# Narrower GpSimd roots, a later evacuation of an expert's result, and a fifth slot of split weights in a two-block float32 transformer kernel

## The chip, the cores and the metric

The kernel runs on one core of one Trainium2 chip. The metric is the device time of one execution in microseconds (us); lower is better. Engines: TensorE (PE, its weight loads PEld) multiplies, VectorE (DVE) and ScalarE (ACT) work elementwise and can read the accumulator PSUM, GpSimd (POOL) works elementwise in SBUF, SyncE (SP) issues most DMAs.

## The reference, cut to what matters

256 tokens of width 1024 pass through a first block (two layers of SwiGLU, a mixer of RWKV and retention heads, SwiGLU) and a second block (two layers of a mixer, cross attention to a memory, a mixture of 16 experts). Everything is float32.

```
def rms_norm(x, gain, eps=NORM_EPS):
    y = xf * lax.rsqrt(jnp.mean(xf * xf, axis=-1, keepdims=True) + eps)
def layer_norm(x, g, b):
    y = (xf - mu) * lax.rsqrt(var + LN_EPS) * g + b
def grouped_moe(...):                      # top 2 of 16 experts for each token
    for e in range(N_EXPERTS):
        he = jax.nn.silu(xt @ w_gate[e]) * (xt @ w_up[e])      # 1024 -> 512
        y = y + combine[:, e:e + 1] * (he @ w_down[e])         # 512 -> 1024
```

The first block has seven RMS norms of whole rows (three a layer and a final one). Inside a layer there are also roots for the key vectors (8 heads of 2 tiles, 16 columns), for the retention heads (8 columns) and for the RWKV heads of each tile (8 columns). The second block has six layer norms and one norm over 8 groups of 2 tiles (16 columns).

## The kernel before, in words

**Rows and columns.** The 256 tokens are two tiles (NT = 2) of 128 partitions. The root of a row norm is therefore 2 columns of 128: one value for each tile and partition. A head norm of one tile is RH = 8 columns.

**Split weights.** Each float32 matmul is done as three: a weight block `raw` (128 x 1024, 512 KB) is rounded by ACT to `whi`, DVE subtracts it from `raw` to give `wlo`, and PE multiplies `whi` with the high part of the data, `wlo` with the high part and `whi` with the low part. SP loads the next `raw` block when DVE is done with an old one.

**Roots.** DVE puts the variances into `rs_in` (16 columns) and raises `rs_asked`; GpSimd computes `rs_in ** -0.5` over all 16 columns into `rs_out` and raises `rs_given`; DVE waits for that in `rsqrt(n)` and scales. 22 such roots run in a fixed order: RSQ = 7 in each of two layers (0: first norm, 1: mixer norm, 2: keys, 3: retention heads, 4 and 5: RWKV heads of tile 0 and 1, 6: second feed-forward norm), then the final norm, the group norm, and six layer norms. In `rms` DVE does nothing while it waits; in `layer_norm` it does two scalar_tensor_tensor operations of its own in the meantime. After a norm PE transposes the normed rows (`turn_rows`), ACT and DVE evacuate them as `xTh` and `xTl`, and the next matmuls start. While a norm runs, PE executes `keep_busy`, a number of matmuls on zeros, ahead of `turn_rows` in its queue.

**Experts.** In each layer of the second block three experts are computed over all tokens and the other NR = 13 over their own tokens only (CAPS: at most 128, 104, 88, ... 32 rows). For those 13 the weights come in NC = 156 chunks: for round i four chunks `up` and four chunks `gate` of expert i, then four chunks `down` of expert i - 1. PE's order in round i is: up(i), `scatter(i - 2)` (which adds an expert's result to the tokens), gate(i), down(i - 1), `turn_e(i)` (transposes of the hidden rows). Split chunks go through NW = 4 slots (three of `whi`/`wlo`, and `w3h`/`w3l`); ACT's split of chunk n waits until PE has used chunk n - NW. ACT and DVE run one program each, in the same order (`split_e`, `silu_e`/`gated_e`, `hidden_e`, `out_e`):

```
                    if i < NR:
                        if i:
                            split_e()
                            if i > 1:
                                out_e(i - 2)
                            split_e()
                            if i == 1:
                                silu_e(0)
                            hidden_e(i - 1)
                        for _ in range(6):
                            split_e()
```

`out_e(i - 2)` copies the down result of expert i - 2 from two PSUM banks into `outh` (stored in `xTh`) and, on DVE, the low half into `outl` (in `xTl`); it needs the last down chunk of the round before. `hidden_e(i - 1)` does the same with the transposed hidden rows (`hTh`, `hTl`) and needs `turn_e(i - 1)`.

Of the kernel before, what the change touches and what calls it, by code (L numbers as in the profile page):

```python
# [8 lines left out]
F32R = mybir.dt.float32r  # L9
BF16 = mybir.dt.bfloat16  # L10
I32 = mybir.dt.int32
ALU = mybir.AluOpType
# [4 lines left out]
P = 128  # L17
D = 1024
S = 256
NT = S // P  # L20
# [51 lines left out]
UNIT_BANKS = (0, 1, 2, 3, 5, 6)  # L72
TURN_BANKS = (0, 1, 2, 3, 5, 6, 7)
NC = 12 * NR
NRAW, NW = 6, 4
UB, GB = 4, 5
POOLS = (2, 4, 8, 16)

# [60 lines left out]
def both_blocks(nc, A, out):  # L139
    ctx = ExitStack()  # L140
    with ctx:
# [51 lines left out]
        xgl = at("xgl", [P, KB, SLOTS], F32R, offset=RB_at)  # L193
        w3h = at("w3h", [P, 1024], F32R, offset=tl_at)
        w3l = at("w3l", [P, 1024], F32R, offset=tl_at + 4 * 1024)
        outh = xTh[:].rearrange("p k s -> p (k s)")[:, 0:D]
        outl = xTl[:].rearrange("p k s -> p (k s)")[:, 0:D]
        gsf, hrows = (b[:].rearrange("p j s -> p (j s)") for b in (gs, h32))
# [240 lines left out]

        def e_w(n):  # L440

            return (w3h[:], w3l[:]) if n % NW == 3 else (whi[:, n % NW], wlo[:, n % NW])

        def hold(eng, signal, value):

# [194 lines left out]
        @block.gpsimd  # L640
        def _(pool):
            pool.wait_ge(setup, 3)

            def rsqrt(n):
                pool.wait_ge(rs_asked, n + 1)
                nc.gpsimd.tensor_tensor(rs_out[:], rs_in[:], neg_half[:], ALU.pow).then_inc(rs_given, 1)  # L646

            with pool.Fori(0, DEPTH) as l:
                for n in range(2):
                    rsqrt(RSQ * l + n)  # L650

                nc.gpsimd.memset(prev[0:1, 0], 0.0).then_inc(zero_row, 1)
                rsqrt(RSQ * l + 2)

                for t in range(NT):
                    for lev in range(6):
                        for hf in range(2):
                            hs = slice(4 * hf, 4 * hf + 4)
                            if lev == 0:

                                pool.wait_ge(L_ready, 16 * l + 8 * t + 4 * hf + 4)
                                if t:

                                    pool.wait_ge(q_psum, 24 * l + 12)
                            else:

                                pool.wait_ge(q_psum, 24 * l + 12 * t + 2 * lev - 2 + hf + 1)
                                if lev == 1:
                                    pool.wait_ge(t_ready, 24 * l + 12 * t + hf + 1)
                            mask = tab[:, T_LEV + lev * P:T_LEV + (lev + 1) * P]  # L670
                            nc.gpsimd.tensor_tensor(Aoff[:, hs], Lm[:, hs, 0:P], mask.unsqueeze(1).to_broadcast([P, 4, P]),  # L671
                                                    ALU.mult).then_inc(aoff_ready, 1)
                    rsqrt(RSQ * l + 3 + t)
                for n in range(5, RSQ):
                    rsqrt(RSQ * l + n)
            with pool.Fori(RSQ * DEPTH, RSQ * DEPTH + 8) as n:
                rsqrt(n)

        @block.scalar
        def _(act):  # L680
# [45 lines left out]
            def experts(l):  # L726
# [32 lines left out]
                for i in range(NR + 1):  # L759
                    if i < NR:  # L760
                        if i:
                            split_e()
                            if i > 1:
                                out_e(i - 2)
                            split_e()
                            if i == 1:
                                silu_e(0)
                            hidden_e(i - 1)
                        for _ in range(6):
                            split_e()  # L770
                        if i:
                            split_e()
# [249 lines left out]
        def _(dve):  # L1022
# [494 lines left out]
            def experts(l):  # L1517
# [119 lines left out]
                for i in range(NR + 1):  # L1637
                    if i < NR:
                        if i:
                            split_e()  # L1640
                            if i > 1:
                                out_e(i - 2)
                            split_e()
                            if i == 1:
                                gated_e(0)
                            hidden_e(i - 1)
                        for c in range(6):
                            split_e()
                            if i == 0 and c == 1:
                                add(ND - 1)  # L1650
# [729 lines left out]
```

## Time and profile before

| | |
|---|---|
| median of 3 runs | 2846.18 us (2845.74 to 2848.23) |
| the profiled execution | 2848.95 us, its span 2847.1 us |
| PE, DVE, ACT, POOL busy | 90%, 58%, 41%, 5% of the span |
| granted TensorE clock, mean | 0.956 of full speed |
| DMA | 460 MB, 162 GB/s over the span |

A row of a timeline is: start in us, duration in us, engine, line, operation, out<-in, count, and in square brackets the idle time before it with what ended it. The span starts at 0.

### The profile page before, as it was taken

The page shows a single profiled execution, that of the slowest core. Times are in us where ns is not written, and L with a number is a line of the kernel's source. Part 1 is how long each engine was busy: PE and PEld are TensorE (multiplying, and loading weights), DVE is VectorE, ACT ScalarE, POOL GpSimd, SP SyncE. Part 2 cuts the span into 40 slices and gives each one's busy share as a digit, 9 for nine tenths or more (in the row PEclk, how much of TensorE's full clock was granted, in tenths as well). Part 3 has the DMA queues.
Part 4 walks back from the last instruction along what each step waited for, and adds up shares of the span by engine and source line. Part 5 has one row for each costly group of instructions (what it writes and reads, how often), then busy time and mean ns, then how long its engine had stood idle before and what let it go on. Part 6 is the DMA issues. An engine that isn't in the chain of part 4 may idle for free.

```text
span 2847.1 us, 39605 instructions
## 1 busy us (share of the span) xinstructions
PE 2561.4 (90%) x14872; PEld 2068.0 (73%) x14872; DVE 1650.0 (58%) x1993; ACT 1153.6 (41%) x1338; POOL 137.4 (5%) x76
## 2 busy tenths in 40 slices
PE   8998888999999888899997889999997877999996
PEld 7987786898898778689885767985443665985443
DVE  5555754554555575455543446667776445667776
ACT  4543312343454331244331323446664321446663
POOL 0000131000000022100000000000000000000000
PEclk9999999999999999999998899999998998999998
DMA  6674201666466520166652323668885422568884
GB/s 212 179 219 141 91 1 30 177 190 179 139 186 199 162 70 1 37 185 184 183 156 85 119 74 114 178 211 305 293 290 192 132 89 60 149 207 297 296 288 168
DMA packets 387417, 460.37 MB, mean 162 GB/s; under 512 B 18534, under 2 KB 272978, under 8 KB 387154
## 3 DMA queue, kind: packets, MB, share of 16 engines
q1 hardware_dynamic: 382384, 448.64, 50.0%
q10 hardware_dynamic: 4898, 9.95, 1.2%
q8 instruction: 83, 1.36, 0.2%
q14 instruction: 52, 0.43, 0.0%
HBM read 453.83 MB, written 1.05 MB: 160 GB/s over the span
## 4 chain that ended last, share of the span: by engine, by line
issue 86%; PE 9%; DVE 2%; POOL 2%; DMA 1%; ACT 0%; ACTq 0%; POOLq 0%; DVEq 0%
PE PS L1951 1%; PE PS L1953 1%; PE PS L1952 1%; POOL rs_out L646 1%; PE PS L2079 1%; POOL solve_b L671 1%; PE PS L2089 1%; DMA RA<-proj 1%; PE PS L2088 1%; PE PS L2062 0%; PE PS L2063 0%; PE PS L2067 0%; DVE solve_a L1282 0%; DVE wlo L1135 0%; PE PS L2120 0%
## 5 line engine op out<-in xcount | busy, mean ns | idle before, releaser
L1084 DVE TENSOR_TENSOR wlo<-raw,whi 128x1024 fp32r<-128x1024 f32 x336 | 410.2, 1225 | 392.6 <-ACT whi L696 391.9
L696 ACT ACTIVATE whi<-raw 128x1024 fp32r<-128x1024 f32 x336 | 355.3, 1060 | 537.0 <-PE PS L1759 361.4
L1757 PE MATMUL PS<-xTh,whi 128*128 128x256 f32 x1792 | 508.7, 284 | 1.7 <-ACT xgh L1011 1.7
L1758 PE MATMUL PS<-xTl,whi 128*128 128x256 f32 x1792 | 507.7, 283 | 0.0
L1759 PE MATMUL PS<-xTh,wlo 128*128 128x256 f32 x1792 | 507.6, 283 | 0.0
L1757 PEld LDWEIGHTS PS<-xTh,whi 128*128 128x128 f32 x1792 | 344.4, 192 | 7.3 <-issue 3.2
L1758 PEld LDWEIGHTS PS<-xTl,whi 128*128 128x128 f32 x1792 | 344.4, 192 | 4.1
L1759 PEld LDWEIGHTS PS<-xTh,wlo 128*128 128x128 f32 x1792 | 344.2, 192 | 0.0
L1612 DVE TENSOR_TENSOR wlo<-raw,whi 128x1024 fp32r<-128x1024 f32 x234 | 280.6, 1217 | 71.8 <-ACT whi L739 71.6
L739 ACT ACTIVATE whi<-raw 128x1024 fp32r<-128x1024 f32 x234 | 245.9, 1054 | 96.1 <-PE PS L1862 78.0
L1951 PE MATMUL PS<-whi,xTh 128*128 128x416 f32 (+2 forms) x544 | 212.6, 391 | 39.5 <-DVE xTl L1064 18.9
L1953 PE MATMUL PS<-whi,xTl 128*128 128x416 f32 (+2 forms) x544 | 207.1, 381 | 0.0
L1952 PE MATMUL PS<-wlo,xTh 128*128 128x416 f32 (+2 forms) x544 | 206.8, 380 | 0.0
L1078 DVE TENSOR_TENSOR wlo<-raw,whi 128x1024 fp32r<-128x1024 f32 (+2 forms) x92 | 106.6, 1177 | 153.5 <-ACT whi L707 152.1
L646 POOL TENSOR_TENSOR rs_out<-rs_in,neg_half 128x16 f32<-128x16 f32 x22 | 71.4, 3244 | 2521.1 <-DVE rs_in L1355 1329.3
L1773 PE MATMUL PS<-whi,hTh 128*128 128x512 f32 x448 | 178.3, 398 | 10.4 <-DVE wlo L1084 10.4
L1774 PE MATMUL PS<-wlo,hTh 128*128 128x512 f32 x448 | 177.7, 397 | 0.0
L1775 PE MATMUL PS<-whi,hTl 128*128 128x512 f32 x448 | 176.5, 394 | 0.0
L1860 PE MATMUL PS<-whi,xgh 128*36 128x512 f32 (+11 forms) x312 | 127.0, 407 | 43.9 <-DVE wlo L1612 43.8
L707 ACT ACTIVATE whi<-raw 128x1024 fp32r<-128x1024 f32 (+2 forms) x92 | 90.8, 1016 | 179.5 <-PE PS L1953 122.6
L1951 PEld LDWEIGHTS PS<-whi,xTh 128*128 128x128 f32 x544 | 106.7, 196 | 65.2 <-issue 28.4
L1729 PE MATMUL PS<-zero 128*128 128x512 bf16 x536 | 124.0, 391 | 10.7 <-issue 9.0
(424 smaller groups left out, 4452.9 us busy)
## 6 DMA issues: line engine op xcount, KB each, us to landing
raw<-in_l_e_gate_dram SPq DMA_DIRECT2D x128, 512.0 KB, 4.7
raw<-in_l_e_up_dram SPq DMA_DIRECT2D x128, 512.0 KB, 5.8
raw<-in_l_e_down_dram SPq DMA_DIRECT2D x128, 512.0 KB, 5.3
raw<-in_ffn_w_gate_dram SPq DMA_DIRECT2D x88, 512.0 KB, 5.0
raw<-in_ffn_w_up_dram SPq DMA_DIRECT2D x88, 512.0 KB, 6.1
raw<-in_ffn_w_down_dram SPq DMA_DIRECT2D x88, 512.0 KB, 3.4
raw<-in_w_in_dram SPq DMA_DIRECT2D x64, 416.0 KB, 3.9
raw<-in_l_xkv_dram SPq DMA_DIRECT2D x32, 512.0 KB, 3.8
```

The source lines that it names most:

```text
L696: nc.scalar.activation(whi[:, m], raw[:, m, j], ACT.Copy).then_inc(hi_done[m], 1)
L739: nc.scalar.activation(e_w(n)[0], e_raw(n), ACT.Copy).then_inc(e_hi, 1)
L1084: nc.vector.tensor_tensor(wlo[:, m], raw[:, m, j], whi[:, m].bitcast(F32), ALU.subtract).then_inc(lo_done[m], 1)
L1612: TTop(e_w(n)[1], e_raw(n), e_w(n)[0].bitcast(F32), ALU.subtract).then_inc(e_lo, 1)
L1757: mm(out_, whi[:, m, ks], xTh[:, k, :], start=(k == 0), stop=False)
L1758: mm(out_, whi[:, m, ks], xTl[:, k, :], start=False, stop=False)
L1759: last = mm(out_, wlo[:, m, ks], xTh[:, k, :], start=False, stop=(k == KB - 1))
L1773: mm(out_, hTh[:, j, ts], whi[:, 2, ns], start=(opens is not None), stop=False, skip_group_check=True)
L1774: mm(out_, hTh[:, j, ts], wlo[:, 2, ns], start=False, stop=False, skip_group_check=True)
L1951: mm(out_, of[0][:, k, ts], whi[:, at[c], ws], start=(k == 0), stop=False)
L1952: mm(out_, of[0][:, k, ts], wlo[:, at[c], ws], start=False, stop=False)
L1953: last = mm(out_, of[1][:, k, ts], whi[:, at[c], ws], start=False, stop=(k == KB - 1))
```

## The change

1. GpSimd's `rsqrt(n, c0, c1)` takes the root only over the columns that the norm has: 2 for each row norm and layer norm (13 roots), 8 for retention and RWKV heads (6 roots), 16 as before for the keys and the group norm (3 roots).
2. In the order of ACT and DVE, `out_e(i - 2)` moves from behind the first `up` split of round i to behind the third; `hidden_e(i - 1)`, still behind the second, now comes before it.
3. NW is 5: a fifth slot `w4h`/`w4l` of split weights lies where `xn` is (which the experts don't use).

```
-NRAW, NW = 6, 4
+NRAW, NW = 6, 5
+        w4h = at("w4h", [P, 1024], F32R, offset=xn_at)
+        w4l = at("w4l", [P, 1024], F32R, offset=xn_at + 4 * 1024)
-            return (w3h[:], w3l[:]) if n % NW == 3 else (whi[:, n % NW], wlo[:, n % NW])
+            if n % NW < 3:
+                return whi[:, n % NW], wlo[:, n % NW]
+            return (w3h[:], w3l[:]) if n % NW == 3 else (w4h[:], w4l[:])
...
-            def rsqrt(n):
+            def rsqrt(n, c0, c1):
                 pool.wait_ge(rs_asked, n + 1)
-                nc.gpsimd.tensor_tensor(rs_out[:], rs_in[:], neg_half[:], ALU.pow).then_inc(rs_given, 1)
+                nc.gpsimd.tensor_tensor(rs_out[:, c0:c1], rs_in[:, c0:c1], neg_half[:, c0:c1], ALU.pow).then_inc(rs_given, 1)
                 for n in range(2):
-                    rsqrt(RSQ * l + n)
+                    rsqrt(RSQ * l + n, 0, NT)
-                rsqrt(RSQ * l + 2)
+                rsqrt(RSQ * l + 2, 0, 16)
-                    rsqrt(RSQ * l + 3 + t)
-                for n in range(5, RSQ):
-                    rsqrt(RSQ * l + n)
-            with pool.Fori(RSQ * DEPTH, RSQ * DEPTH + 8) as n:
-                rsqrt(n)
+                    rsqrt(RSQ * l + 3 + t, 0, RH)
+                rsqrt(RSQ * l + 5, RH, 2 * RH)
+                rsqrt(RSQ * l + 6, 0, NT)
+            rsqrt(RSQ * DEPTH, 0, NT)
+            rsqrt(RSQ * DEPTH + 1, 0, 16)
+            with pool.Fori(RSQ * DEPTH + 2, RSQ * DEPTH + 8) as n:
+                rsqrt(n, 0, NT)
...
                         if i:
                             split_e()
-                            if i > 1:
-                                out_e(i - 2)
                             split_e()
                             if i == 1:
                                 silu_e(0)
                             hidden_e(i - 1)
-                        for _ in range(6):
+                            split_e()
+                            if i > 1:
+                                out_e(i - 2)
+                        for _ in range(5 if i else 6):
                             split_e()
```

(The last piece stands twice, for ACT as here and for DVE with `gated_e`.)

DVE in round i = 8 of layer 0, where the results have 52 rows and the hidden rows 192 columns; `wlo`, `w3l`, `w4l` are splits of chunks, `xTl` is `out_e(6)`, `hTl` is `hidden_e(7)`. Before:

```order
806 L1618 SCALAR_TENSOR_TENSOR h<-gs,par,PS 48x512
807 L1612 TENSOR_TENSOR wlo<-raw,whi 128x1024
808 L1612 TENSOR_TENSOR w3l<-raw,w3h 128x1024
809 L1612 TENSOR_TENSOR wlo<-raw,whi 128x1024
810 L1629 TENSOR_TENSOR xTl<-PS,xTh 52x1024
811 L1612 TENSOR_TENSOR wlo<-raw,whi 128x1024
812 L1624 TENSOR_TENSOR hTl<-PS,hTh 128x192
813 L1612 TENSOR_TENSOR wlo<-raw,whi 128x1024
814 L1612 TENSOR_TENSOR w3l<-raw,w3h 128x1024
```

The same place on DVE with the change:

```order
803 L1625 SCALAR_TENSOR_TENSOR h<-gs,par,PS 48x512
804 L1619 TENSOR_TENSOR wlo<-raw,whi 128x1024 x3
805 L1619 TENSOR_TENSOR w3l<-raw,w3h 128x1024
806 L1631 TENSOR_TENSOR hTl<-PS,hTh 128x192
807 L1619 TENSOR_TENSOR w4l<-raw,w4h 128x1024
808 L1636 TENSOR_TENSOR xTl<-PS,xTh 52x1024
809 L1619 TENSOR_TENSOR wlo<-raw,whi 128x1024 x3
```

Behind the hidden rows' gating (the first row) DVE now does four splits (down 2, down 3, up 0, up 1) before it turns to the hidden rows, then the third up split, then the result; before, the result stood between up 0 and up 1. ACT's queue moved in the same way. Before:

```order
496 L744 ACTIVATE gs<-PS 48x512
497 L739 ACTIVATE whi<-raw 128x1024
498 L739 ACTIVATE w3h<-raw 128x1024
499 L739 ACTIVATE whi<-raw 128x1024
500 L752 ACTIVATE xTh<-PS 52x1024
501 L739 ACTIVATE whi<-raw 128x1024
502 L748 ACTIVATE hTh<-PS 128x192
503 L739 ACTIVATE whi<-raw 128x1024
```

And ACT with the change:

```order
493 L750 ACTIVATE gs<-PS 48x512
494 L745 ACTIVATE whi<-raw 128x1024 x3
495 L745 ACTIVATE w3h<-raw 128x1024
496 L754 ACTIVATE hTh<-PS 128x192
497 L745 ACTIVATE w4h<-raw 128x1024
498 L758 ACTIVATE xTh<-PS 52x1024
499 L745 ACTIVATE whi<-raw 128x1024 x3
```

The copy of the result (`xTh`) stands two places later, and the copy of the hidden rows is the first of the two that waits for PE. On GpSimd no instruction is added or moved; the last block of its program reads, with the change:

```order
74 L650 TENSOR_TENSOR rs_out<-rs_in,neg_half 128x2
75 L650 TENSOR_TENSOR rs_out<-rs_in,neg_half 128x16
76 L682 UNCONDITIONAL_BRANCH
77 L682 ISA
78 L650 TENSOR_TENSOR rs_out<-rs_in,neg_half 128x2
79 L682 REGISTER_ALU
80 L682 COMPARE_AND_BRANCH
```

Before, one loop of eight roots of 128x16 stood there; now the final norm and the group norm are outside the loop of the six layer norms.

## Rows read from the trace of the kernel before

**Rows 1.** The page: busy time and share of the span by engine.

```profile
PE 2561.4 (90%) x14872; PEld 2068.0 (73%) x14872; DVE 1650.0 (58%) x1993; ACT 1153.6 (41%) x1338; POOL 137.4 (5%) x76
```

**Rows 2.** Waits of PE: line, releaser, total us, times, longest us.

```profile
PE PS L1860 <- DVE wlo L1612: 43.8, 27, 2.5
```

**Rows 3.** Tile rs_out: its root (ns min/median/max) and who waited (us, times).

```profile
L646 POOL TENSOR_TENSOR rs_out<-rs_in,neg_half x22: 2900/2915/3867, 8.8 to 2835.3; 128x16 f32<-128x16 f32 x22
...
  DVE xn L1046: 18.6, 6
  DVE x L1363: 9.2, 6
```

**Rows 4.** Timeline, the second layer norm.

```profile
1703.99 2.60 DVE L1359 SCALAR_TENSOR_TENSOR x<-x,par,gain 128x1024 f32<-128x1024 f32 x2
...
1708.11 2.48 DVE L1363 SCALAR_TENSOR_TENSOR x<-x,rs_out,gain 128x1024 f32<-128x1024 f32 x2 [1.53 <-POOL rs_out L646]
1710.70 3.35 PE L1740 MATMUL PS<-tab,x 128*128 128x128 f32 x16 [2.64 <-DVEq L1377]
```

**Rows 5.** Timeline, transposes after two feed-forward norms.

```profile
508.21 2.40 PE L1740 MATMUL PS<-tab,xn 128*128 128x128 f32 x16 [2.35 <-DVEq L1069]
...
719.89 2.45 PE L1740 MATMUL PS<-tab,xn 128*128 128x128 f32 x16 [3.93 <-DVEq L1069]
```

**Rows 6.** Timeline, the mixer norm of layer 0.

```profile
222.88 1.97 PE L1740 MATMUL PS<-tab,xn 128*128 128x128 f32 x16 [1.08 <-DVEq L1152]
...
223.58 2.07 ACT L690 ACTIVATE xTh<-PS 128x512 fp32r<-128x512 f32 x4 [11.89 <-PE PS L1740]
...
224.89 2.48 DVE L1064 TENSOR_TENSOR xTl<-PS,xTh 128x512 fp32r<-128x512 f32 x4
...
227.70 0.45 PE L1951 MATMUL PS<-whi,xTh 128*128 128x416 f32 x1 [2.85 <-DVE xTl L1064]
```

**Rows 7.** Timeline, transposes after layer 1's mixer norm and the first norm.

```profile
928.27 1.97 PE L1740 MATMUL PS<-tab,xn 128*128 128x128 f32 x16 [0.69 <-DVEq L1152]
...
16.95 1.91 PE L1740 MATMUL PS<-tab,xn 128*128 128x128 f32 x16
```

**Rows 8.** Timeline, other operations of GpSimd.

```profile
0.25 0.10 POOL L2370 MEMSET const-float32-0.0<- 128x1 f32 x1 [0.25 <-issue]
...
337.39 1.28 POOL L671 TENSOR_TENSOR solve_b<-RA,tab 128x512 f32<-128x512 f32 x1 [29.01 <-DVE RA L1271]
```

**Rows 9.** Timeline, the RWKV head norm of tile 1, layer 0.

```profile
464.22 0.69 DVE L1255 TENSOR_TENSOR xn<-xn,rs_out 128x512 f32<-128x512 f32 x1 [2.79 <-POOL rs_out L646]
...
467.93 3.04 PE L1740 MATMUL PS<-tab,xn 128*128 128x128 f32 x16 [2.30 <-DVEq L1328]
```

**Rows 10.** Timeline, the end of round 7 and the start of round 8, layer 0.

```profile
2057.23 1.04 ACT L739 ACTIVATE whi<-raw 128x1024 fp32r<-128x1024 f32 x1
...
2058.69 1.22 DVE L1612 TENSOR_TENSOR wlo<-raw,whi 128x1024 fp32r<-128x1024 f32 x1
...
2060.61 0.45 PE L1891 MATMUL PS<-tab,h 48*128 48x48 f32 x4
2060.72 1.02 ACT L752 ACTIVATE xTh<-PS 52x1024 fp32r<-52x1024 f32 x1 [2.45 <-PE PS L1881]
...
2061.77 1.22 DVE L1629 TENSOR_TENSOR xTl<-PS,xTh 52x1024 fp32r<-52x1024 f32 x1 [1.86 <-ACT xTh L752]
...
2062.59 0.31 ACT L748 ACTIVATE hTh<-PS 128x192 fp32r<-128x192 f32 x1
2064.17 0.43 PE L1860 MATMUL PS<-whi,xgh 128*44 128x512 f32 x1 [1.59 <-DVE wlo L1612]
```

**Rows 11.** Windows: busy us (instructions) by engine, granted clock, DMA share, GB/s.

```profile
205.00:212.00 7.00, 4.54 (x15) 3.24 (x13) 2.27 (x2) 2.85 (x3) 0.00 (x0) 0.80 1.00 365
...
1612.00:1616.00 4.00, 2.36 (x13) 1.96 (x10) 4.00 (x6) 3.07 (x5) 0.00 (x0) 0.51 0.45 133
...
2000.00:2050.00 50.00, 46.59 (x198) 25.14 (x199) 39.30 (x37) 32.33 (x35) 0.00 (x0) 1.00 0.85 290
```

More of the change, by code:

```diff
@@ L1640, in experts @@
                             split_e()
-                            if i > 1:
-                                out_e(i - 2)
                             split_e()
@@ L1646, in experts @@
                             hidden_e(i - 1)
-                        for c in range(6):
+                            split_e()
+                            if i > 1:
+                                out_e(i - 2)
+                        for c in range(5 if i else 6):
                             split_e()
```

## The prediction

> **What bounds the kernel now.** The page comes first: PE is busy for 90% of the span, POOL for 5% [rows 1]. So the time is PE's queue and the gaps in it, and a change pays where it shortens a gap of PE or lets it work at the full clock. The waits of PE, read next, put one entry on top: line L1860, the first matmul of a chunk in the experts' stage, waits for DVE's split (`wlo`), 43.8 us in 27 waits, none over 2.5 us [rows 2]. The other gaps that matter here lie at the norms, where PE waits for the normed rows before it can transpose. The view of the tile `rs_out` shows what a root costs and who waits for it: a root takes 2.90 us at least, 3.87 at most, whether 2 or 16 of its columns are wanted; DVE waits 18.6 us in six RMS norms (3.1 each) and 9.2 us in the six layer norms (1.53 each) [rows 3]. The page's chain of waits is nearly all "issue" here, and gave nothing.
>
> A root on the chain is worth something only if PE has run out of zero matmuls (`keep_busy`) when the rows come. The timeline around each norm tells that: PE was idle 2.64 us before the transposes of the layer norm shown [rows 4], 2.35 and 3.93 us at two feed-forward norms [rows 5], 1.08 us at the mixer norm of layer 0 [rows 6], 0.69 us at that of layer 1, and not at all at the very first norm [rows 7].
>
> **Change 1, the price of a narrow root.** The trace has no pow of 2 or 8 columns, so I bound it. From below: all proportional, 2.90 x 2/16 = 0.36 us. From above: a GpSimd multiply of 512 columns takes 1.28 us in all and a memset of one column 0.10 us [rows 8], so what an instruction costs before its first column is at most 1.28; then a column of pow costs (2.90 - 1.28)/16 = 0.10 and two columns cost 1.28 + 0.20 = 1.48 us. I take the fixed part near the memset's, 0.10, since 512 columns of the multiply must fit in the rest: a column is 0.175, two columns 0.45, eight 1.5. An RMS root of 2 columns then ends 2.4 us earlier (between 1.4 and 2.5), a head root of 8 columns about 1.5 earlier (0.8 to 1.6).
>
> **Layer norms, six.** DVE runs 2.60 us of its own beside the root and then waits 1.53 [rows 4]. A root of 0.45 us disappears behind the 2.60; what is left of 1.53 is a semaphore, so 1.4 us each. PE is idle for 2.64 us there, so it takes over all of it; the last layer norm has only the output's DMA behind it. 6 x 1.4 = **8.4 us**. Even the upper bound of 1.48 us is hidden, so this term doesn't hang on the price of a column.
>
> GpSimd and DVE disturb each other: the roots beside DVE's two-input operations are the ones of 3.87 us, the undisturbed ones 2.90 [rows 3], so 2.60 us of DVE's work [rows 4] cost the root some 0.97. [...] By the rows it slows down by a third and no more; were it held, it would end 0.45 us after DVE's 2.60 and the term would be 6 x 1.0 = 6 instead of 8.4 us.
>
> **RMS norms, seven.** DVE has nothing to do but wait, so it gains the whole 2.4 us; what arrives at PE depends on `keep_busy`.
> - Feed-forward norms: PE idle 2.35 (twice) and 3.93 us [rows 5], behind them DVE's splits and evacuations, which start when DVE is free. 3 x 2.4 = 7.2. The first norm of the kernel: the transposes start without any wait [rows 7], gain 0.
> - Mixer norm of layer 0: the transposes can come 1.08 earlier, at 221.80. The first `xTh` is done 0.70 + 0.6 later, at 223.1, then DVE's four `xTl` of 0.62 each (2.48 in all) end at 225.6, and with the 0.33 that lay between, PE starts at 225.95 instead of 227.70 [rows 6]: 1.75. The 1.08 is not the limit, because DVE's two splits ahead of `xTl` held that chain. Layer 1 has 0.69 in place of 1.08 [rows 7]: 1.35. The final norm of block one, the same shape, taken between them: 1.5. Together 4.6.
> - RWKV head norm of tile 1, twice: DVE waits 2.79, PE 2.30 us [rows 9], the root saves 1.5: 3.0. Retention's root and that of tile 0 have no one waiting; nothing. The keys' and the groups' roots are unchanged.
>
> Sum of change 1: 8.4 + 7.2 + 4.6 + 3.0 = **23.2 us**.
>
> **Changes 2 and 3, the experts' rounds.** A round takes some 21.5 us (12 chunks, a scatter, a turn and the wait), and in each of rounds 2 to 12 of both layers (22) PE waits once, before the second up chunk: 1.59 us in the row shown [rows 10]. 22 such waits are 35.0 us, and the other five of the 27 share what is left of the 43.8 [rows 2]; I count 1.6 each. The reason stands in rows 10 and in the order: DVE, in order, can't split up 1 before it has evacuated the result, which it gets at 2061.77, although it had split up 0 at 2058.69 and then waited 1.86 us.
>
> With the change, by hand from the same durations (a DVE split 1.22, the next one 1.14 later; ACT's next 0.95 later): ACT splits up 1 at 2058.2, DVE right behind up 0, 2059.8 to 2061.05, before PE wants it (2062.4). This needs slot up 1, free with NW = 5 when down 0 is used, with 4 when down 1 is, both in time; the fifth slot alone would not remove the wait, since the order holds it. Then `hidden_e(7)` has to wait for `turn_e`, 2060.61 + 0.45: ACT 2061.15, 0.31 long, DVE to 2061.85. ACT splits up 2 to 2062.4, DVE 2062.45 to 2063.7; PE, through with up 1 at 2063.8, goes on at once. ACT's copy of the result runs 2062.3 to 2063.3, DVE's 2063.6 to 2064.8; DVE's split of up 3 follows, 2064.75 to 2065.97. PE is through with up 2 at 2065.2: a wait of **0.8 us** before up 3 is what is late next. The scatter behind up 3 wants `outl`, there since 2064.8. Gain per round 1.6 - 0.8 = 0.8; 22 x 0.8 = **17.6 us**. Bounds: all of it gone, 35; and, if half a microsecond more goes to evacuations that run late, 22 x 0.3 = 6.6. The move costs no instruction.
>
> The next bound in these rounds would be DMA. A round moves 12 chunks of 512 KB, 6.3 MB; the steady part runs at 290 GB/s with a DMA share of 0.85, and 365 GB/s are reached at a share of 1.00 [rows 11]. At 20.7 us a round wants 304 GB/s, a share of 0.9. ACT is never late for a block now, and I leave this at 0.
>
> **Sum.** 23.2 + 17.6 = 40.8 us. The profiled execution took 2848.95, 1.85 beyond its span: 2808.1 for one like it; it is 2.8 above the median of the runs, and for the median I predict 2846.2 - 40.8 = **2805 us**.
>
> **The clock, on either side.** [...] Shorter gaps should spare some of these stretches, while a shift of everything by 41 us may place others; I take 0 in the sum and -8 to +6 in the range.
>
> **Rivals.**
> - *The root costs the same whatever its width* (a fixed cost inside pow that multiply and memset don't have). Change 1 gives 0 and 17.6 remain: 2829. Against it: the extra 0.97 us beside DVE looks like a price per access. 7%.
> - *The experts' wait only moves* (DVE is late by as much before up 3, or for the scatter), changes 2 and 3 give 0 to 8: 2815 to 2823. For it: DVE is busy 39.3 of 50 us there [rows 11] and its order stays strict; against it, the hand schedule. 8%.
> - *More than the sum*: the wait goes altogether or the clock stays up behind most norms, 8 to 15 us more: 2790 to 2797. 9%.
> - *Slower, by DMA*: with splits further ahead the blocks are asked for in bursts and land late, so that PE waits for loads. The place is the 22 rounds; it decides when a round loses more than change 1 gains, 23.2/22 = 1.05 us beyond its 21.5, that is below 6.3 MB / 22.55 us = 279 GB/s. At 22.8 us a round the time would be 2846 - 23 + 22 x 1.3 = 2852. Against it: 290 GB/s at a share of 0.85 now, and blocks are freed earlier, not later. 2%.
> - *Not doing what it says*: PE is held elsewhere at the norms and rounds, within 5.7 us (0.2%, about what a measurement of this kernel can tell) of 2846. 2%.
>
> The forecast has 72%, at 2798 to 2812.
>
> **How the numbers follow.** The likeliest case gives 2805. For 8 in 10 the range has to take in most of the rivals on both sides: 2790 (a clock that helps, or a wait that goes entirely) to 2826 (one of the two halves missing for the most part). Faster by over 0.2%: all but the last two and a remainder, 0.95; within it 0.03; slower 0.02.
>
> **What would show it.** Roots of 128x2 near 0.45 us undisturbed and near 0.6 beside DVE, of 128x8 near 1.5; DVE's wait for `rs_out` at 0.7 in the RMS norms and gone in the layer norms; PE's idle before those transposes at 1.2 instead of 2.64. In the rounds: turn to turn 20.7 us instead of 21.5, the wait before up 1 gone and one near 0.8 before up 3, DMA share at 0.9. Wrong would be the sum if the two-column root took over 1.5 us, if ACT showed waits for `raw` from DMA, or if more of PE's time after the norms were granted half its clock.

## The result, and the profile after

| | before | after |
|---|---|---|
| median of 4 runs | 2845.96 us (2839.48 to 2848.23) | 2799.48 us (2795.83 to 2800.71) |
| profiled execution, its span | 2848.95, 2847.1 us | 2798.82, 2797.0 us |
| granted TensorE clock, mean | 0.956 | 0.961 |

The ratio is 0.9833, 95% interval 0.9816 to 0.9849: the change takes off 46.5 us (1.7%), where 40.8 were forecast. 2799.5 lies inside the range 2790 to 2826. Of the nine executions of the kernel before that ran beside e5 to e8 (below), one took 12048 us; it counts in their median and in no ratio.

The page after, busy time by engine (it answers to [rows 1]): by its records PE is busy 21 us less and idle 29 us less, and POOL has lost 36 us. Not all of the 21 us is work saved: after has 76 records of matmuls fewer, all of zero matmuls, though the change adds and removes none, and the busy time of these groups is some 10 us lower. By this estimate the idle time has shrunk by nearer 39 us.

```profile
PE 2540.2 (91%) x14796; PEld 2060.2 (74%) x14872; DVE 1649.2 (59%) x1993; ACT 1143.8 (41%) x1338; POOL 101.3 (4%) x76
```

The waits of PE in the experts' up and gate chunks, after (line, releaser, total us, times, longest), for the one row of [rows 2]: the split is now in three tiles, and 12.5 + 4.9 + 3.7 = 21.1 us stand in place of 43.8. 22.7 us of waiting are gone.

```profile
PE PS L1868 <- DVE wlo L1619: 12.5, 14, 2.5
...
PE PS L1868 <- DVE w4l L1619: 4.9, 6, 1.8
...
PE PS L1868 <- DVE w3l L1619: 3.7, 6, 0.7
```

The tile `rs_out` after, for [rows 3]: what a root costs (ns, min/median/max) and who waits for it (us, times). DVE's wait is 0.88 us in an RMS norm instead of 3.1, and no layer norm waits.

```profile
L650 POOL TENSOR_TENSOR rs_out<-rs_in,neg_half x22: 695/1648/3390, 8.7 to 2786.7; 128x2 f32<-128x2 f32 x13, 128x8 f32<-128x8 f32 x6, 128x16 f32<-128x16 f32 x3
...
  DVE xn L1053: 5.3, 6
  DVE xn L1262: 3.1, 2
  DVE proj L1463: 3.0, 1
  DVE x L1053: 0.8, 1
```

One timeline row for each width where DVE is idle when the root starts (start, duration, engine, line, operation; beside the second DVE later runs operations with one input from SBUF and one from PSUM):

```profile
216.82 0.70 POOL L650 TENSOR_TENSOR rs_out<-rs_in,neg_half 128x2 f32<-128x2 f32 x1 [207.43 <-DVE rs_in L1048]
...
374.64 1.64 POOL L650 TENSOR_TENSOR rs_out<-rs_in,neg_half 128x8 f32<-128x8 f32 x1
...
1467.66 2.90 POOL L650 TENSOR_TENSOR rs_out<-rs_in,neg_half 128x16 f32<-128x16 f32 x1 [61.52 <-DVE rs_in L1461]
```

2, 8 and 16 columns take 0.69 to 0.70, 1.64 and 2.90 us: a straight line, (2.90 - 0.69) / 14 = 0.158 a column and 0.375 ahead of the first. The prediction had 0.175 and 0.10.

The second layer norm after, for [rows 4]. The root still takes 1.66 us here, yet L1370 follows L1366 with no wait, since 1.66 is well hidden behind 2.60. PE is idle 1.15 us instead of 2.64, and its 16 transposes take 1.97 us instead of 3.35, at a granted clock of 1.00 instead of 0.56. The shorter transposes gain nothing here: from their start to the first matmul on the transposed rows it is 4.90 us, and was 4.91, since the copies by ACT and DVE lie between. The gain is the 1.49 us by which they start earlier.

```profile
1681.43 2.60 DVE L1366 SCALAR_TENSOR_TENSOR x<-x,par,gain 128x1024 f32<-128x1024 f32 x2
1681.60 1.66 POOL L650 TENSOR_TENSOR rs_out<-rs_in,neg_half 128x2 f32<-128x2 f32 x1 [95.98 <-DVE rs_in L1362]
1684.07 2.48 DVE L1370 SCALAR_TENSOR_TENSOR x<-x,rs_out,gain 128x1024 f32<-128x1024 f32 x2
1686.66 1.97 PE L1748 MATMUL PS<-tab,x 128*128 128x128 f32 x16 [1.15 <-DVEq L1384]
```

The feed-forward norms after, for [rows 5]: at the first PE's 2.35 us of idleness are gone but for 0.14, at the second 1.93 of 3.93 are left.

```profile
508.83 1.97 PE L1748 MATMUL PS<-tab,xn 128*128 128x128 f32 x16
...
715.35 1.97 PE L1748 MATMUL PS<-tab,xn 128*128 128x128 f32 x16 [1.93 <-DVEq L1076]
```

The mixer norm of layer 0 after, for [rows 6]. The transposes start without a wait, and PE then waits 2.17 us for `xTl`, as it waited 2.85 before.

```profile
221.23 1.91 PE L1748 MATMUL PS<-tab,xn 128*128 128x128 f32 x16
...
222.50 2.48 DVE L1071 TENSOR_TENSOR xTl<-PS,xTh 128x512 fp32r<-128x512 f32 x4
...
225.31 0.55 PE L1959 MATMUL PS<-whi,xTh 128*128 128x416 f32 x1 [2.17 <-DVE xTl L1071]
```

The end of round 7 and the start of round 8 after, for [rows 10]. No wait is left before up 1 or up 2; the one before up 3, the last row, is 0.60 us. `hTl` comes first, then the split of up 2 (`w4l`), then the result (`xTl`), then the split of up 3.

```profile
2032.62 0.44 PE L1899 MATMUL PS<-tab,h 48*128 48x48 f32 x4
...
2033.46 0.36 DVE L1631 TENSOR_TENSOR hTl<-PS,hTh 128x192 fp32r<-128x192 f32 x1 [0.42 <-ACT hTh L754]
...
2034.40 1.23 DVE L1619 TENSOR_TENSOR w4l<-raw,w4h 128x1024 fp32r<-128x1024 f32 x1 [0.59 <-ACT w4h L745]
...
2035.55 1.21 DVE L1636 TENSOR_TENSOR xTl<-PS,xTh 52x1024 fp32r<-52x1024 f32 x1
...
2036.68 3.48 DVE L1619 TENSOR_TENSOR wlo<-raw,whi 128x1024 fp32r<-128x1024 f32 x3
...
2037.94 0.42 PE L1868 MATMUL PS<-whi,xgh 128*44 128x512 f32 x1 [0.60 <-DVE wlo L1619]
2053.06 0.44 PE L1899 MATMUL PS<-tab,h 44*128 44x44 f32 x4
```

From turn to turn that is 2053.06 - 2032.62 = 20.44 us. The turn before that one stands in this row, 20.51 us earlier; the rounds differ a little from one to the next.

```profile
2012.11 0.45 PE L1899 MATMUL PS<-tab,h 52*128 52x52 f32 x4
```

The same interval as the 20.44 was 21.48 us before, from the turn in [rows 10] to the next, which stands in this row of the timeline of before:

```profile
2082.09 0.45 PE L1891 MATMUL PS<-tab,h 44*128 44x44 f32 x4
```

Windows after, in the experts' rounds (columns as in [rows 11]): DMA's share is 0.89 to 0.90, at 306 to 315 GB/s, and PE is busy 48.0 to 48.4 of 50 us, where it was 46.6.

```profile
1960.00:2010.00 50.00, 48.36 (x209) 26.73 (x208) 38.59 (x36) 31.65 (x36) 0.00 (x0) 1.00 0.90 315
2010.00:2060.00 50.00, 48.00 (x207) 24.20 (x206) 40.29 (x39) 34.08 (x39) 0.00 (x0) 1.00 0.89 306
```

The rounds can be timed as a whole: in each layer, from the first turn to the thirteenth and last, both layers added. This leaves the norms and what the clock does elsewhere out of it, and it repeats within 0.2 us between kernels whose rounds are alike:

| kernel (the experiments are below) | us, both layers |
|---|---|
| before | 509.1 |
| e3, fifth slot alone | 509.0 |
| e2, new order alone | 485.9 |
| e4, order and slot | 486.1 |
| after | 485.9 |
| e10, result one place earlier | 490.5 |
| e5, late scatter | 467.6 |
| e9, late scatter, four slots | 467.6 |

Only the order changes the rounds. (e1, the roots alone, has 510.5: one of its rounds was granted a clock of 0.93 and took 1.5 us longer.)

### The profile page after: what moved, and what is told of

Same layout as the page of the kernel before. It is cut to its first block, busy times and chain, and to the rows that moved or that the text cites. A ratio compares the mean times of both kernels' runs of the same rounds, so it can differ in the third digit from the quotient of the medians.

```text
span 2797.0 us, 39521 instructions
## 1 busy us (share of the span) xinstructions
PE 2540.2 (91%) x14796; PEld 2060.2 (74%) x14872; DVE 1649.2 (59%) x1993; ACT 1143.8 (41%) x1338; POOL 101.3 (4%) x76
## 3 DMA queue, kind: packets, MB, share of 16 engines
HBM read 453.83 MB, written 1.05 MB: 163 GB/s over the span
## 4 chain that ended last, share of the span: by engine, by line
PE 65%; issue 16%; DVE 13%; ACT 4%; POOL 1%; DMA 1%; ACTq 0%; DVEq 0%; POOLq 0%; PEldq 0%; SPq 0%
PE PS L1765 6%; PE PS L1767 6%; PE PS L1766 6%; PE PS L1959 3%; PE PS L1781 3%; PE PS L1961 3%; PE PS L1782 3%; PE PS L1960 3%; PE PS L1783 3%; PE PS L1868 2%; PE PS L1870 2%; PE PS L1869 2%; DVE wlo L1619 2%; ACT whi L745 1%; PE PS L1737 1%
## 5 line engine op out<-in xcount | busy, mean ns | idle before, releaser
L1091 DVE TENSOR_TENSOR wlo<-raw,whi 128x1024 fp32r<-128x1024 f32 x336 | 410.1, 1224 | 391.5 <-ACT whi L702 390.7
L702 ACT ACTIVATE whi<-raw 128x1024 fp32r<-128x1024 f32 x336 | 355.4, 1060 | 540.9 <-PE PS L1767 362.7
L1619 DVE TENSOR_TENSOR wlo<-raw,whi 128x1024 fp32r<-128x1024 f32 x188 | 222.1, 1217 | 35.8 <-ACT whi L745 35.7
L745 ACT ACTIVATE whi<-raw 128x1024 fp32r<-128x1024 f32 x188 | 190.1, 1051 | 45.2 <-PE PS L1870 18.1
L1142 DVE TENSOR_TENSOR wlo<-raw,whi 128x832 fp32r<-128x832 f32 (+1 forms) x80 | 83.2, 1062 | 88.7 <-ACT whi L803 86.8
L1737 PE MATMUL PS<-zero 128*128 128x512 bf16 x472 | 116.4, 389 | 15.5 <-issue 9.6
L650 POOL TENSOR_TENSOR rs_out<-rs_in,neg_half 128x2 f32<-128x2 f32 (+2 forms) x22 | 35.1, 1594 | 2498.4 <-DVE rs_in L1362 1307.8
```

Of the source, the lines that this page charges most:

```text
L702: nc.scalar.activation(whi[:, m], raw[:, m, j], ACT.Copy).then_inc(hi_done[m], 1)
L1091: nc.vector.tensor_tensor(wlo[:, m], raw[:, m, j], whi[:, m].bitcast(F32), ALU.subtract).then_inc(lo_done[m], 1)
L1619: TTop(e_w(n)[1], e_raw(n), e_w(n)[0].bitcast(F32), ALU.subtract).then_inc(e_lo, 1)
```

## Where the 50.1 us between the two profiled executions lie

**At the norms.** I took the distance from each root's start to the first matmul that PE starts behind the transposes and their copies, in both timelines. At the first norm and the feed-forward norms this is a zero matmul that waits for DVE's `xTl`; at the final norm it is the first one on `xTh`, behind a second set of transposes:

| place | before | after | gained | forecast |
|---|---|---|---|---|
| first norm | 12.03 | 11.69 | 0.3 | 0 |
| mixer norm, layers 0, 1 | 10.46, 10.47 | 8.49, 8.48 | 4.0 | 3.1 |
| final norm of block one | 14.80 | 11.18 | 3.6 | 1.5 |
| RWKV head norm, tile 1 | 12.35, 12.34 | 11.08, 11.11 | 2.5 | 3.0 |
| feed-forward norms | 10.43, 10.64, 10.61 | 8.22, 8.43, 8.22 | 6.8 | 7.2 |
| layer norms 1 to 3 | 11.61, 11.45, 11.84 | 10.11, 9.96, 10.34 | 4.5 | 4.2 |
| layer norms 4 to 6 | 11.71, 10.93, 11.76 | 10.12, 8.97, 10.30 | 5.0 | 4.2 |

(The last is to the end of the span.) Together 26.7 us, against 23.2.

**In the rounds** 22.7 us of waits, against 17.6; by the table of turns it is 23.2. **The rest** is 50.1 - 26.7 - 22.7 = 0.7 us, the net of the clock elsewhere, and that is a sum of large parts. The same stage of the first block, from the keys' root to the retention root, the same 375 matmuls, in windows of before and of after:

```profile
304.99:370.65 65.66, 54.57 (x375) 49.60 (x374) 42.20 (x54) 15.93 (x21) 19.43 (x13) 0.95 0.12 41
```

```profile
304.55:374.64 70.09, 59.00 (x375) 53.13 (x374) 42.21 (x54) 15.92 (x21) 19.58 (x14) 0.88 0.12 38
```

It took 4.4 us longer after the change, with DVE, ACT and POOL as busy as before and the granted clock at 0.88 instead of 0.95. Another stage, from 1483.86 us of before on, gave 4.6 us back (120.94 to 116.31), its clock going from 0.87 to 0.93.

## Experiments

The kernel before ran on the same chip as each experiment: median 2850.13 us beside e1 to e4, 2852.24 beside e5 to e8, 2849.34 beside e9 and e10. Ratios are to it.

**e1_roots_only**: before with change 1 alone, the column ranges of the roots.

```diff
-                nc.gpsimd.tensor_tensor(rs_out[:], rs_in[:], neg_half[:], ALU.pow).then_inc(rs_given, 1)
+                nc.gpsimd.tensor_tensor(rs_out[:, c0:c1], rs_in[:, c0:c1], neg_half[:, c0:c1], ALU.pow).then_inc(rs_given, 1)
```

> Only the narrow roots (change 1), the experts' stage as before. Theory of the prediction: -23 us against before, so about 2823. Rival that the extra gain seen with the whole change (46.5 us against 40.8 forecast) belongs to the norms, by fewer stretches at half clock: -28 or more. In the trace: roots of 128x2 0.69 us, beside DVE's layer norm work 1.66 us; DVE's wait in the RMS norms 0.9 us and none in the layer norms.

Measured: 2822.93 us (2813.15 to 2827.07), ratio 0.9910 (0.9894 to 0.9925), 26 us less (21 to 30). PE still waits for the splits in the rounds:

```profile
PE PS L1862 <- DVE wlo L1614: 43.6, 26, 2.5
```

So the roots bring their 26 us alone and don't touch the rounds. The interval takes in both the forecast of 23 and the rival's 28, so the time alone doesn't say whether the norms gained more than forecast; the table of the norms does.

**e2_order_only**: before with the new order of `out_e`, four slots.

```diff
                             split_e()
-                            if i > 1:
-                                out_e(i - 2)
                             split_e()
...
                             hidden_e(i - 1)
-                        for _ in range(6):
+                            split_e()
+                            if i > 1:
+                                out_e(i - 2)
+                        for _ in range(5 if i else 6):
```

> Only the evacuation of an expert's result moved behind the third up split, four slots, wide roots. Theory: the order held the wait and the fifth slot is not needed for it, so this gives the whole gain of the experts' stage, -17.6 by the prediction, -22 by the 1.0 us a round seen with the whole change: 2823 to 2829. Rival: the gain needs the fifth slot, since with four ACT can split up 1 only when down 1 is used: less than half of that, -10 or less.

Measured: 2826.84 us (2819.58 to 2830.51), ratio 0.9923 (0.9907 to 0.9938), 22 us less (18 to 27). With four slots up 3 always lies in `w3h`/`w3l`, so its wait has a row of its own, free of others:

```profile
PE PS L1862 <- DVE w3l L1613: 13.5, 22, 0.7
...
PE PS L1862 <- DVE wlo L1613: 7.0, 4, 2.5
```

22 waits, 0.61 us each: exactly one in each of the 22 rounds, and 0.6 rather than the 0.8 of the prediction.

**e3_slot_only**: before with the fifth slot, the order untouched.

```diff
-NRAW, NW = 6, 4
+NRAW, NW = 6, 5
```

> Only the fifth slot, old order, wide roots. Theory: nothing, within 2 us of before, with the wait before the second up chunk still 1.6 us in 22 rounds, since ACT and DVE are held by the result's evacuation in their own order and not by a slot. Rival: a slot more lets DVE run ahead elsewhere in the round and takes a third of the wait or more: -7 or more.

Measured: 2851.30 us (2841.33 to 2856.61), ratio 1.0006 (0.9992 to 1.0020): nothing. PE's waits are what they were, 28.3 + 8.5 + 6.8 = 43.6 us, while ACT, a slot further ahead, has come upon the transfers:

```profile
PE PS L1864 <- DVE wlo L1616: 28.3, 16, 2.5
...
PE PS L1864 <- DVE w4l L1616: 8.5, 6, 1.8
...
PE PS L1864 <- DVE w3l L1616: 6.8, 4, 1.8
```

```profile
ACT whi L743 <- DMA raw<-in_l_e_down_dram: 28.4, 21, 3.2
```

**e4_order_and_slot**: before with both, that is changes 2 and 3 (the two diffs above).

> The order and the fifth slot, wide roots. Theory: as the order alone, -17.6 to -22, within 2 us of that kernel, and the sum with the roots-only kernel gives the whole change, -46. Rival of an interaction (the slot pays only with the new order): 5 us or more better than the order alone.

Measured: 2822.91 us (2821.54 to 2828.82), ratio 0.9909 (0.9893 to 0.9925), 26 us less (21 to 30). It is 4 us faster than e2 in the median, with overlapping intervals; that is no effect of the slot, since the rounds of the two take 485.9 and 486.1 us. e1 and e4 together would be 0.9910 x 0.9909 = 0.982; the whole change measured 0.983 (0.9816 to 0.9849). Within their intervals the two halves add up.

**e5_late_scatter**: after, with the result evacuated yet later, behind the first gate chunk's split, and PE's scatter moved behind the gate chunks.

```diff
                         up_or_gate(i, UB, 0 if i else 2, 4 if i else 2)
-                        if i > 1:
-                            scatter(i - 2)
...
                         assert n == gate_end(i)
+                        if i > 1:
+                            scatter(i - 2)
```

```diff
-                            split_e()
-                            if i > 1:
-                                out_e(i - 2)
-                        for c in range(5 if i else 6):
+                        for c in range(6):
                             split_e()
...
+                            if i > 1 and c == 2:
+                                out_e(i - 2)
```

(The second piece on ACT and DVE alike. c = 0 and 1 are up 2 and up 3, c = 2 is the first gate chunk: the result is evacuated behind that one's split.)

> The changed kernel, with the evacuation of the result moved on behind the first gate split and PE's scatter(i - 2) moved from between up and gate to behind gate. Theory: the 0.6 us that PE still waits before the fourth up chunk is DVE's evacuation standing ahead of that split, so it goes and nothing takes its place, DVE being ahead in the gate chunks: 22 x 0.6 = 13 us under the changed kernel, 20.43 us a round down to 19.85, about 2786. Rival: DVE or DMA are the bound of a round (DMA share 0.9 already) and the wait turns up at another chunk: 0 to 5 us.

Measured: 2780.27 us (2770.66 to 2786.18), ratio 0.9751 (0.9725 to 0.9776), 0.8 percentage points below the changed kernel; in medians 19 us, where 13 were expected. In the rounds of the window PE waits nowhere. Its turns are 19.66 us apart, and the window shows it busy 49.78 of 50 us:

```profile
2013.41 0.45 PE L1897 MATMUL PS<-tab,h 52*128 52x52 f32 x4
...
2033.07 0.44 PE L1897 MATMUL PS<-tab,h 48*128 48x48 f32 x4
```

```profile
1985.00:2035.00 50.00, 49.78 (x218) 27.23 (x216) 39.49 (x39) 32.74 (x38) 0.00 (x0) 1.00 0.93 327
```

The remaining 0.6 us wait was thus the order's as well, and at a DMA share of 0.93 and 327 GB/s PE still waits for no transfer; ACT does three times in the window, for 0.22 to 0.43 us. The gain goes past that wait: 22 x 0.6 = 13, while the same two turns are 20.51 us apart in the changed kernel and 19.66 here, and all rounds together are 18.3 us shorter (485.9 to 467.6), 0.83 each. Most of the difference is in how a wait is counted. After, the last matmul of up 2 stands in this row:

```profile
2036.95 0.39 PE L1870 MATMUL PS<-w4h,xgl 128*44 128x512 f32 x1
```

The first of up 3 starts at 2037.94, 0.99 us later, where the matmuls of a chunk start 0.23 apart. So the late split costs 0.76 us a round, some 17 in 22 rounds, of which the profile, counting from the modelled end of the last matmul, shows 0.60.

**e6_ln_beside**: after, with two tests of what holds GpSimd beside DVE. In layer 0 DVE waits for the root before it starts its own two operations; in layer 1 these become one-tensor operations, which leaves out the multiplication by the gain there.

```diff
+                if k < 3:
+                    rsqrt(ask)
                 for t in range(NT):
...
+                    else:
+                        own(nc.vector.tensor_scalar(x[:, t], x[:, t], aggr[:, t, 0:1], 1.0, ALU.subtract, ALU.mult))
```

> A look at what stands beside the root of a layer norm. The changed kernel, but in the three layer norms of layer 0 DVE waits for the root before its own two operations, and in the three of layer 1 these operations take one tensor from SBUF in place of two (the gain is left out of the product there, so the result is another). [...] Rival: a slowdown in proportion to the root's accesses, which the 2-column root of 1.66 us speaks against; then 0.69 in layer 0 and something between in layer 1. Layer 0's norms should end some 0.9 us later each.

Measured (one execution, 2792.76 us). First rows, layer 0: alone the root takes 0.69 us. Second rows, layer 1: beside two operations with one SBUF input, which run at 0.77 us instead of 1.30, it still takes 1.40 us.

```profile
1576.35 0.69 POOL L650 TENSOR_TENSOR rs_out<-rs_in,neg_half 128x2 f32<-128x2 f32 x1 [113.41 <-DVE rs_in L1362]
1577.16 2.60 DVE L1369 SCALAR_TENSOR_TENSOR x<-x,par,gain 128x1024 f32<-128x1024 f32 x2 [0.89 <-POOL rs_out L650]
...
2242.16 1.53 DVE L1371 TENSOR_SCALAR x<-x,par 128x1024 f32<-128x1024 f32 x2
2242.32 1.40 POOL L650 TENSOR_TENSOR rs_out<-rs_in,neg_half 128x2 f32<-128x2 f32 x1 [86.72 <-DVE rs_in L1362]
```

If only operations with two SBUF inputs held GpSimd, the root would have taken 0.69 us in layer 1 too; its 1.40 us are against that. That DVE is the cause stands: alone, the root takes 0.69 us, beside DVE's pair 1.66. Its place beside DVE's pair is still the better one: in layer 0 the first matmul on the transposed rows comes 11.10, 10.95 and 11.32 us after the root's start, 1.0 us later than in the changed kernel, against 0.9 expected.

**e7_busy_trimmed** and **e8_busy_filled**: after, with a block of 8 zero matmuls less in two places where PE no longer has time for them, and with more of them where it is still idle.

```diff
-                keep_busy(5)
+                keep_busy(4)
...
-            keep_busy(3)
+            keep_busy(2)
```

> The changed kernel with 8 zero matmuls fewer (1.8 us) behind each feed-forward stage and at the start. Theory: at the two mixer norms and the final norm the transposes now start when the zeros end, and DVE's chain behind them is short of full by some 0.2 us each; at the start the raw weights and ACT are the limit. So it gives 0.5 us at the most, and the norm that had idle time before (layer 1's first) gets 1.8 us more of it: no change, within 3 us. Rival: PE's zeros held up the norms by more than the DVE chain shows, -3 to -5 us; or the clock falls more often without them, +3 or more.

Measured: 2799.24 us (2797.98 to 2803.90), ratio 0.9825 (0.9805 to 0.9844), the same as the change itself. The trace shows the terms behind it: at the two mixer norms the distance of the table falls from 8.49 and 8.48 to 8.29 and 8.26 us, the 0.2 expected of each, and at the final norm it grows from 11.18 to 12.27.

```diff
-                keep_busy(4)
+                keep_busy(5)
                 turn_rows(r, x)
...
-                keep_busy(4)
+                keep_busy(5)
                 turn_rows(r + 2, x)
...
                 if l == 0:
+                    keep_busy(6, 7)
                     turn_rows(14, x)
```

> The changed kernel with 8 zero matmuls more (1.8 us) at the five places of block two where PE idles 1.15 us before transposes, and 48 in the 9.8 us hole after layer 0's experts. Theory: idle time ahead of a norm's transposes is a reason for the half clock behind them, so the granted clock behind these norms is 1.0 more often: -3 to -8 us. Rival: the light work behind the norm decides and not the hole before it, or the clock falls as often: within 2 us, or slower by the 0.6 us that the zeros overrun at each place, +3.

Measured: 2797.58 us (2792.63 to 2803.83), ratio 0.9822 (0.9798 to 0.9845). The 3 to 8 us that a fuller clock should have brought are not shown. At the second layer norm the idleness is closed:

```profile
1681.89 1.91 PE L1748 MATMUL PS<-tab,x 128*128 128x128 f32 x16
```

But the 19 us from there on were granted the same clock as those of the changed kernel. Windows of e8 and of after:

```profile
1681.00:1700.00 19.00, 16.00 (x96) 15.26 (x95) 9.14 (x12) 5.03 (x7) 0.00 (x0) 0.73 0.26 84
```

```profile
1686.00:1705.00 19.00, 14.98 (x89) 14.70 (x90) 9.33 (x12) 5.03 (x7) 0.00 (x0) 0.73 0.27 84
```

**e9_late_scatter_4**: e5 with four slots.

```diff
-NRAW, NW = 6, 5
+NRAW, NW = 6, 4
```

> The late scatter with four slots of split weights instead of five. Theory: with the order right, the fifth slot still has little to do (order alone and order with slot were 4 us apart, their intervals overlapping): within 5 us of the late scatter with five slots, 2780. Rival: now that a round is 19.7 us and nothing else waits, splits must run further ahead of PE, and four slots bring waits for PE's use back: 5 us or more slower.

Measured: 2779.97 us (2778.20 to 2782.09), ratio 0.9756 (0.9742 to 0.9769), the same as e5. The fifth slot isn't needed there either.

**e10_out_second**: after, with the result evacuated one split earlier, directly behind the hidden rows.

```diff
                             hidden_e(i - 1)
-                            split_e()
                             if i > 1:
                                 out_e(i - 2)
-                        for c in range(5 if i else 6):
+                        for c in range(6):
                             split_e()
```

> The changed kernel with the result's evacuation behind the second up split and the hidden rows, in place of behind the third. By the durations of the trace DVE then has the third split done 1.05 us after PE wants it (evacuation 1.22, split 1.22 in a row behind the hidden rows), against 0.6 before the fourth chunk with the change: 22 x 0.45 = 10 us slower than the changed kernel, about 2809, and still some 12 us better than the old place. Rival: it is enough that up 1 no longer stands behind the evacuation, and the exact place doesn't matter: within 3 us of the changed kernel.

Measured: 2803.87 us (2795.65 to 2811.27), ratio 0.9827 (0.9813 to 0.9841), which can't be told from the change. The trace can: the wait has moved to up 2 and is 0.82 us long in the row below (1.05 by my hand schedule), and the turns, at 2024.77 and 2045.47, are 20.70 us apart, the same two in the changed kernel 20.51. All rounds together are 4.6 us longer (490.5 against 485.9), half of the 10 expected and within the noise of the runs. So the exact place does matter, and the rival (within 3 us) is out.

```profile
2049.62 0.43 PE L1866 MATMUL PS<-w4h,xgh 128*44 128x512 f32 x1 [0.82 <-DVE w4l L1618]
```

## Why the prediction was right, and where it was off

- **The bound and the two halves**: right. PE's queue and its gaps set the time; e1 and e4 show that the halves work alone and add up.
- **Fixed part of a root, 0.10 us**: mis-sized, it is 0.375; a two-column root takes 0.69 us, not 0.45, one of eight 1.64, not 1.5. That cost 0.2 at the RMS norms (2.2 instead of 2.4 saved), 0.2 at the head norms, and nothing in the layer norms, where even the 1.66 us beside DVE are hidden behind DVE's 2.60. The rival of a root with one price whatever its width is out.
- **"By the rows it slows down by a third and no more"**: wrong as a mechanism, harmless as a price. If it were a rate, the root of 0.69 us would have taken 0.9 beside DVE; it took 1.66. The 0.97 us of [rows 3] is the same for 16 columns (3.87 - 2.90) and for 2 (1.66 - 0.69). So it was no argument against a root of one price either, as which the prediction used it ("a price per access"). The case weighed beside it, a root held until both of DVE's operations are done, is shown by no run and is wrong too: that root would have ended 0.69 us after DVE's 2.60. It ended at 1683.26, 0.77 us before DVE was through.
- **Layer norms, 8.4 us**: 9.5. The 1.53 us vanish completely (about 1.5 each), and the fifth gained 1.96, of which 1.48 until its transposes start and the rest behind that start, where they take 1.97 us at a granted clock of 1.00 instead of 2.93 at 0.64.
- **Feed-forward norms, 7.2 us**: 6.8. **Mixer norms, 3.1 us**: 4.0. The chain that was forecast is right (transposes as soon as the zero matmuls end, ACT's copy, DVE's four `xTl`); what was mis-sized is when the zeros end, 4.41 and 4.40 us after the root's start, where rows of before gave 4.56 and 4.95. The root saves 2.2 us and 2.0 arrive; the other 0.2 is held by the zeros, as e7 shows. **Final norm, 1.5 us**: 3.6, of which 2.1 until the second transposes; these took 3.43 us before at a granted clock of 0.55 and 1.94 after at 1.00, so 1.5 are the clock's, which the sum had at 0.
- **Rounds, 17.6 us**: 22.7. The direction, the place of the new wait (before up 3, e2's 22 rows) and its cause are right; the term was mis-sized since the new wait is 0.6 us and not 0.8 (22 x 0.2 = 4.4), and since the old one was 1.66 us on the average of the 22 rounds, not 1.6: the row shown has 1.59, those of rounds 2 to 4 have 1.77 to 1.85. DVE's split of up 3 was to end 5.36 us after the turn and PE did start on it at 5.32; PE, in the hand schedule through with up 2 4.6 us after the turn, needs 4.72. A difference of two chains counts every 0.1 us 22 times.
- **"The fifth slot alone would not remove the wait"**: right (e3), and it adds nothing to the order: the rounds of e2 and e4, and those of e5 and e9, take the same time within 0.2 us.
- **DMA left at 0**: right. The share rose to 0.9 as forecast, but the sign that I had named as an alarm appeared, with no loss: ACT waits for the `raw` of down chunks 12.8 us in 21 waits, the row below and two small ones for the other slots, and is still early enough. In e2, with four slots, these waits are 1.2 us, and the rounds are as long. Here the wait of an engine that runs ahead cost nothing.

```profile
ACT whi L745 <- DMA raw<-in_l_e_down_dram: 10.4, 14, 2.8
```

- **Clock 0 in the sum**: as a net near enough (0.7 us gained outside the norms and rounds), but that is luck, since single stages moved by over 4 us either way; inside the norms some 2 us more are the clock's (final and fifth layer norm). The other terms were too low by 3.5 + 5.1 = 8.6 us in the profiled execution, which by itself would be the rival "more than the sum". The medians differ by 46.5 and not 50.1, so that 5.7 us of the error are left in them. The range's -8 to +6 us for the clock were an estimate of mine, and no run shows that idleness ahead of a norm brings half the clock behind it. What was measured: 1612 to 1616 us were granted 0.51 [rows 11], and after the change 1.00 stood at the transposes of four layer norms where 0.54 to 0.64 had, but closing the idleness in e8 gained nothing that its time or its windows show (0.73 either way).

## What to carry to other kernels

An engine that works in order and serves two consumers should take the item whose producer finishes late behind all those that are ready; then look at what is late next and move again: the second move (e5) took 18 us off the rounds where the first had taken 23. Price a narrow instruction by a fixed part and a part per column, and check whether its narrow case is hidden anyway, which makes the price irrelevant. Don't read buffer depth as the limit before the order has been ruled out: here one more slot was worth nothing in three pairs.

## What the runs showed of the hardware

**Beside DVE a root ended about when it would have, had it started at the end of the DVE instruction then running.** From the timelines:

| root | DVE's instruction then running, its end | root's end | behind it | undisturbed |
|---|---|---|---|---|
| 16 columns (before, 1704.16) | 1.30 us, 1705.29 | 1708.02 | 2.73 | 2.90 |
| 2 columns (after, 1681.60) | 1.30 us, 1682.73 | 1683.26 | 0.53 | 0.69 |
| 8 columns (after, 466.02) | 0.68 us, 466.53 | 468.03 | 1.50 | 1.64 |
| 16 columns (after, 304.55) | 0.69 us, 305.18 | 307.94 | 2.76 | 2.90 |
| 2 columns (e6, 2242.32) | 0.77 us, one input, 2242.93 | 2243.72 | 0.79 | 0.69 |

(1.30 and 0.77 are half of the pairs' 2.60 and 1.53.) In the first four rows the root ends 0.14 to 0.17 us before its own time has passed behind that one instruction, whatever its width. What DVE starts meanwhile did not hold it again: the fourth row is the keys' root of 3.39 us, and five more DVE operations with two SBUF inputs start while it runs, at 305.10, 305.74, 306.34, 307.05 and 307.66.

```profile
304.55 3.39 POOL L650 TENSOR_TENSOR rs_out<-rs_in,neg_half 128x16 f32<-128x16 f32 x1 [85.50 <-DVE rs_in L1181]
```

e6's row fits less well: it is 0.10 us over instead of 0.16 under, and the root ends 0.03 us after DVE's second operation does, so that a second hold isn't ruled out there.

What in the chip holds the root is not shown. The rows show for how long: 0.97 us beside operations with two SBUF inputs of 1.30 us, for both widths, 0.37 and 0.49 us beside such ones of 0.68 and 0.69 us (2.01 - 1.64, 3.39 - 2.90), and 0.71 us (1.40 - 0.69) beside operations with one SBUF input of 0.77 us. That GpSimd disturbs DVE in turn, as the prediction has it, is not seen here: the pair takes 2.60 us with a root beside it (rows of the layer norm after) and 2.60 without (e6, layer 0).

**A GpSimd pow of 128 partitions** costs 0.375 us and 0.158 us a column, by its 0.69, 1.64 and 2.90 us at 2, 8 and 16 columns (after).

**The granted clock differed where the instructions did not.** In one stage, from the keys' root to the retention root, it was 0.95 before and 0.88 after, worth 4.4 us; in another, from 1483.86 us of before on, 0.87 and 0.93, worth 4.6 us. Closing the idleness ahead of one set of transposes left the next 19 us at 0.73 (e8). At four layer norms the 16 transposes took 1.97 us at a clock of 1.00 after 1.15 us of idleness (after) and 2.93 to 3.54 us at 0.64 to 0.54 after 2.64 us (before), but that makes no rule: behind the group norm they took 3.67 us at 0.50 before (1569.64) and 1.97 at 1.00 after (1549.09), with 1.16 us of idleness both times. Executions of one kernel differ by 4 to 16 us. What sets these phases stays open; the effects of e8 and e10, under 6 us, can't be told from them by time alone.
